# One-hot rows for the gate matmuls: both indices compared in one VectorE instruction and the gate multiplied in by ScalarE, in every second gate step

## The reference, cut to what matters

```
cand = v1 + v2 (16 x 16 sums per head);  top, pos = top_k(cand, 16)
eidx = i1 * 128 + i2 at pos;  gate = softmax(top)          # 8 heads x 16 experts per token
act  = gelu(u[eidx] . h, exact) * gate
y    = sum over the 128 chosen experts of act * v[eidx]
```

## Time and profile before

| | |
|---|---|
| time, median of 3 runs | 1566.21 us (1565.37 to 1568.46) |
| the profiled execution's own time | 1565.81 us |
| its span in the trace | 1563.7 us |
| granted TensorE clock, mean | 0.996 of full speed |
| busy over the span | PE 97%, PEld 82%, DVE 90%, ACT 38%, POOL 32% |
| iterations 27 to 50, where the gate steps lie | about 533 to 721 us of the span |

### The profile page before, as it was taken

How to read it: one execution, slowest core, us unless ns; L and a number is a source line. 1 busy time by engine, 2 the same in 40 slices (tenths; PEclk the granted TensorE clock), 3 DMA queues, 4 the chain that set the end, 5 groups by cost and what they waited for, 6 DMA issues and landing times.

```text
span 1563.7 us, 23267 instructions
## 1 busy us (share of the span) xinstructions
PE 1512.8 (97%) x8404; PEld 1281.7 (82%) x8404; DVE 1401.7 (90%) x2988; ACT 596.5 (38%) x968; POOL 493.3 (32%) x422
## 2 busy tenths in 40 slices
PE   7999999899999999999999999999999999999996
PEld 5455654788899999999898999999999899787885
DVE  5887987799999999995999999999999999989997
ACT  3104431521555445543333333333333333334343
POOL 1000000232010411010555565555555555343330
PEclk9999999999999999999999999999999999999998
DMA  9864232230465788789999999999999999999993
GB/s 325 287 217 148 101 138 59 81 98 38 136 212 154 261 262 256 251 278 313 408 396 396 402 401 410 407 397 398 399 407 404 385 402 375 362 406 377 398 391 121
DMA packets 180570, 455.71 MB, mean 291 GB/s; under 512 B 15020, under 2 KB 81700, under 8 KB 178280
## 3 DMA queue, kind: packets, MB, share of 16 engines
q1 hardware_dynamic: 113600, 231.84, 41.2%
q0 software_dynamic: 57632, 209.78, 34.9%
q10 hardware_dynamic: 9224, 12.62, 2.4%
HBM read 421.63 MB, written 32.25 MB: 290 GB/s over the span
## 4 chain that ended last, share of the span: by engine, by line
PE 55%; DVE 13%; DMA 4%; issue 2%; ACT 1%; DVEq 0%; SPq 0%; POOL 0%; ACTq 0%; POOLq 0%
PE peer_psum L1656 13%; PE peer_psum L1660 7%; PE peer_psum L1716 6%; PE peer_psum L1723 6%; PE peer_psum L1731 6%; PE peer_psum L1668 4%; PE peer_psum L1703 3%; PE peer_psum L1720 3%; PE peer_psum L1726 3%; DVE s_all L1807 2%; DMA s_all<-in_peer_v 2%; PE peer_psum L1641 1%; DVE s_all L1902 1%; DVE s_in L1906 1%; DVE s_all L1904 1%
## 5 line engine op out<-in xcount | busy, mean ns | idle before, releaser
L1656 PE MATMUL peer_psum<-hH,hi_slots 128*128 128x320 f32 x1024 | 307.3, 314 | 5.1 <-ACT hi_slots L1599 2.1
L1656 PE MATMUL peer_psum<-hL,hi_slots 128*128 128x320 f32 x1024 | 302.0, 309 | 0.0
L1527 POOL DMA_INDIRECT hT<-in_peer_u,eidx x128 | 146.6, 1145 | 292.0 <-DVE dots L1798 251.5
L1563 ACT ACTIVATE hi_slots<-s_all 128x1024 fp32r<-128x1024 f32 x128 | 135.9, 1062 | 189.2 <-PE peer_psum L1731 172.0
L1527 POOL DMA_INDIRECT hT<-in_peer_v,eidx x128 | 149.6, 1169 | 177.6 <-DVE s_all L1807 164.7
L1656 PEld LDWEIGHTS peer_psum<-hH,hi_slots 128*128 128x128 f32 x1024 | 192.6, 188 | 9.7 <-issue 5.2
L1656 PEld LDWEIGHTS peer_psum<-hL,hi_slots 128*128 128x128 f32 x1024 | 192.6, 188 | 3.1 <-issue 0.2
L1660 PE MATMUL peer_psum<-hH,lo_slots 128*128 128x320 f32 x1024 | 171.2, 309 | 2.1 <-DVE lo_slots L1845 2.1
L1935 DVE TENSOR_TENSOR lo_slots<-s_all,hi_slots 128x1024 fp32r<-128x1024 f32 x128 | 156.3, 1221 | 17.5 <-ACT hi_slots L1563 15.9
L1807 DVE SCALAR_TENSOR_TENSOR s_all<-hT,coef,s_all 128x1024 f32<-128x1024 f32 x126 | 161.3, 1280 | 3.3 <-DMA hT<-in_peer_v,eidx 2.9
L1660 PEld LDWEIGHTS peer_psum<-hH,lo_slots 128*128 128x128 f32 x1024 | 156.6, 188 | 5.1 <-DVE lo_slots L1845 2.6
(11 more groups left out here) (318 smaller groups left out, 2856.6 us busy)
## 6 DMA issues: line engine op xcount, KB each, us to landing
ring<-in_peer_u SPq DMA_DIRECT2D x128, 512.0 KB
s_all<-in_peer_v SPq DMA_DIRECT2D x128, 512.0 KB
gate_table<-lot SPq DMA_DIRECT2D x16, 1280.0 KB, 7.1
lot<-gate_table SPq DMA_DIRECT2D x16, 1280.0 KB
gelu_table<-s_all ACTq DMA_DIRECT2D x56, 160.0 KB
s_in<-gelu_table SPq DMA_DIRECT2D x56, 160.0 KB
x_sb<-in_w_mod POOLq DMA_DIRECT2D x8, 1024.0 KB, 8.2
lot<-in_peer_wq SPq DMA_DIRECT2D x8, 1024.0 KB, 5.6
```

Source lines behind the costliest of these rows:

```text
L1527: pool.indirect_dma_start(rows_of(j), None, A[table][0], bass.IndirectOffsetOnAxis(eidx[:, k:k + 1], 0)).then_inc(rows_in[j % RG], 16)
L1563: func(H[:, slot_of(w), :], vb[:, w % RING, :], ACT.Copy).then_inc(v_hi, 1)
L1656: mm(ps[:, bank, 0:TD], H[:, b, c * P:(c + 1) * P], h[:, c, T0:T], start=(c == 0 and h is hH), stop=False)
```

## The change

In every second gate step (m odd, 40 of 80), VectorE makes one comparison over 4 x 2 x 128 columns for both indices and no multiplication. ScalarE then multiplies the four rows of the second index by the gate, in place, with four instructions over 128 columns (`gate_rows`). TensorE's step waits for ScalarE (`act_made`) instead of for VectorE. Of the odd steps, one that is first or second in its iteration gets its `gate_rows` between `lead_high` and `gelu`; every later one gets it right before the `stage_gates` of the step two before it. Secondly, VectorE makes the low parts of blocks 35 to 39 as well. The semaphore `y_sq` is renamed to `act_made` and its later waits are moved up by the 40 counts.

```diff
-LOW_BY_DVE = [n for n in range(LEAD) if 25 <= n < 35 or n >= 40]
+LOW_BY_DVE = [n for n in range(LEAD) if n >= 25]
+def by_act(m):
+    return m % 2 == 1
+BY_ACT = sum(by_act(m) for m in range(GSTEPS))
...
+            def gate_rows(m):
+                b, d0 = m % NHOT, GT * m
+                act.wait_ge(hot_dve, m + 1)
+                for k in range(GT):
+                    ins = func(onehot[:, b, k, 1, :], onehot[:, b, k, 1, :], ACT.Copy, scale=selT[:, 2, d0 + k:d0 + k + 1])
+                ins.then_inc(act_made, 1)
...
                 if it + 1 < LEAD and it + 1 not in LOW_BY_DVE:
                     lead_low(it + 1)
+                for m in STEPS[it][:2]:
+                    if by_act(m):
+                        gate_rows(m)
                 gelu(it, 4 + it % 2)
...
                 for m in STEPS[it]:
+                    if m + 2 in STEPS[it] and by_act(m + 2):
+                        gate_rows(m + 2)
                     stage_gates(m)
...
             def gates(m):
-                pe.wait_ge(hot_dve, m + 1)
+                if by_act(m):
+                    pe.wait_ge(act_made, sum(by_act(k) for k in range(m + 1)))
+                else:
+                    pe.wait_ge(hot_dve, m + 1)
...
             def hot_rows(m):
                 if m >= NHOT:
                     dve.wait_ge(g_full, m - NHOT + 1)
+                if by_act(m):
+                    v.tensor_tensor(onehot[:, b, :, :, :], iota[:].unsqueeze(1).unsqueeze(1).broadcast_to([P, GT, 2, P]),
+                                    selT[:, 0:2, d0:d0 + GT].rearrange("p i t -> p t i").unsqueeze(3).broadcast_to([P, GT, 2, P]),
+                                    ALU.is_equal).then_inc(hot_dve, 1)
+                    return
```

More of the change, by code:

```diff
@@ L1419, in peer_block @@
         (u_turned, half_turned, u_high, u_less, u_low, u_low_dve, ua_high, ua_low, ub_high, ub_low, u_done, s_ready, v_hi, v_lo, v_done, c_done,
-         a_ready, a_hi, a_lo, yc_done, folded, y_sq, out_ready) = (sem(n) for n in (
+         a_ready, a_hi, a_lo, yc_done, folded, act_made, out_ready) = (sem(n) for n in (
              "u_turned", "half_turned", "u_high", "u_less", "u_low", "u_low_dve", "ua_high", "ua_low", "ub_high", "ub_low", "u_done", "s_ready",
-             "v_hi", "v_lo", "v_done", "c_done", "a_ready", "a_hi", "a_lo", "yc_done", "folded", "y_sq", "out_ready"))
+             "v_hi", "v_lo", "v_done", "c_done", "a_ready", "a_hi", "a_lo", "yc_done", "folded", "act_made", "out_ready"))
         def rows_of(j):
@@ L1608, in _ @@
                     for h in range(2):
-                        func(y[:, 1, 0:512], y_of(0, h), ACT.Square, accum_out=stat[:, 0, h:h + 1]).then_inc(y_sq, 1)
-                        act.wait_ge(y_sq, h + 1)
+                        func(y[:, 1, 0:512], y_of(0, h), ACT.Square, accum_out=stat[:, 0, h:h + 1]).then_inc(act_made, 1)
+                        act.wait_ge(act_made, BY_ACT + h + 1)
             act.wait_ge(c_done, 1)
@@ L1620, in _ @@
                         act.wait_ge(folded, h + 1)
-                    func(sq[:], y_of(t, h), ACT.Square, accum_out=stat[:, 0, 2 * i + h:2 * i + h + 1]).then_inc(y_sq, 1)
-                    act.wait_ge(y_sq, 2 * i + h + 1)
+                    func(sq[:], y_of(t, h), ACT.Square, accum_out=stat[:, 0, 2 * i + h:2 * i + h + 1]).then_inc(act_made, 1)
+                    act.wait_ge(act_made, BY_ACT + 2 * i + h + 1)
         @block.tensor
@@ L1987, in _ @@
                 if n == FIN + 2:
-                    dve.wait_ge(y_sq, 2)
+                    dve.wait_ge(act_made, BY_ACT + 2)
                     rstd(0, 1)
@@ L1996, in _ @@
                 for h in range(2):
-                    dve.wait_ge(y_sq, 2 * i + h + 1)
+                    dve.wait_ge(act_made, BY_ACT + 2 * i + h + 1)
                     step.put(v.tensor_tensor(y[:, t, h * 512:(h + 1) * 512], y_of(t, h), gg2[:, h * 512:(h + 1) * 512], ALU.mult))
```

## The result

The changed kernel takes 1572.87 us (median of 7 runs, 1571.28 to 1576.53), the kernel before 1566.21 (7 runs beside it, 1562.58 to 1568.46). The ratio is 1.0038 with a 95% interval of 1.0024 to 1.0051, so it is slower by about 6 us (3.8 to 8.0). Forecast were 1573.9, slower, and a range of 1567 to 1579. The profiled execution took 1572.42, with a span of 1570.4.

What follows compares the result with a forecast made beforehand. TensorE's chain was taken to bound the gate stage, with ScalarE lacking slack inside runs of gate steps. 9.9 + 0.8 - 2.3 - 0.7 = +7.7 us, so 1573.9 us, 0.5% slower; range 1567 to 1579.

Steps and rivals of the forecast that it cites:

- TensorE sets the end, and a faster VectorE buys only its waits.: Gate stage: iteration 42's chain is TensorE alone, 7.18 us; its waits for VectorE are 1.4 us by matmuls, 2.2 by loads.
- Four ScalarE instructions take 1.275 us; the wait for the bank binds.: Gate steps: a group takes 1.275 us, and the third step's load waits for the first step's move out of PSUM.
- The estimate of 1.17 for a group: ScalarE's four multiplications: 0.29 us each by the page's fixed cost, without overlap, making the forecast 1.6 us lower.
- 24 groups cost nothing, 16 cost 9.9.: Gate stage: 24 groups lie in idle time ahead of the Gelu; 16 ahead of a move delay TensorE 9.9 us.
- The lower bound beside it: ScalarE's groups: at 0.94 us a group, each delay is 0.34 us shorter, 4.5 us in all.
- rival (a): ScalarE's groups are short, 0.94 us: delays shrink to 5.4 us, sum +2.9, about 1569 us; chance 0.14.
- Iteration 27, 0.8.: Iteration 27: VectorE begins late, so TensorE's second step gets its rows late; 0.8 us lost, between 0.4 and 1.2.
- VectorE's relief, 0.7.: Mainly iterations 33 and 34: VectorE's shorter odd steps give TensorE 0.7 us back, bounds 0 and 2.2.
- The low parts, -2.3, hidden by the first edit alone.: Blocks 35 to 39: TensorE drops matmuls, gaining 2.3 us; VectorE takes on 5.7 us, covered by 5.8 saved.
- ScalarE loses five copies that it made in idle time; nothing comes of it: Blocks 35 to 39: dropping ScalarE's copies of the low parts was claimed to change nothing.
- What follows the stage moves along.: Behind the gate stage: TensorE waits for `gelu_table` stores, 7.45 us each, issued relative to its progress, so later work shifts along.
- Rival (d): Behind the stage: drained DMA queues return stores sooner, giving back up to half the loss, 1566 to 1570 us; chance 0.11.

Runs made afterwards that it cites:

- e8: The changed kernel with the 16 later groups multiplying only two of four rows, two tokens' gates left out; 0.9978 of the kernel before, stage -2.4 us.
- e1: The changed kernel with only the 24 odd steps that are first or second in their iteration going over ScalarE; 0.9995 of the kernel before.
- e2: The changed kernel with only the 16 odd steps that are third or later in their iteration going over ScalarE; 1.0050 of the kernel before.
- e3: The changed kernel with the groups of an iteration's first four steps all ahead of the Gelu; 1.0037 of the kernel before, stage +3.0 us.
- e4: The changed kernel with each later group behind the move of the step two before it, not ahead; 1.0108 of the kernel before.
- e10: The changed kernel without VectorE's low parts of blocks 35 to 39, first groups ahead of ScalarE's low-part copy; 1.0055 of the kernel before.
- e11: The changed kernel with later groups cut into two halves placed apart, fifth steps and some others left to VectorE; 1.0009 of the kernel before.
- e5: The kernel before with only the low parts of blocks 35 to 39 moved to VectorE; 1.0014 of the kernel before, stage +3.2 us.
- e6: The changed kernel with the low parts of blocks 35 to 39 left to TensorE and ScalarE; 1.0077 of the kernel before, stage +12.0 us.

## Why the prediction was right

The verdict, the size and the mechanism came out, by the steps as they were put:

- *TensorE sets the end, and a faster VectorE buys only its waits.* Shown: VectorE's load fell by 3.8 us in 20 and nothing came of it. With short groups (e8) the most that was gained in the stage is 2.4 us.
- *Four ScalarE instructions take 1.275 us; the wait for the bank binds.* Measured 1.27, and the load 0.12 behind the move's end. The estimate of 1.17 for a group, from the page "VectorE: DVE Perf Modes" of the Trainium skill ("The TRN2 errata"), is 0.1 short by this trace; the 0.29 per instruction agrees with the distance of starts, (1.27 - 0.39) / 3.
- *24 groups cost nothing, 16 cost 9.9.* e1 and e2 show the split. The term of 9.9 was a little large: the clean three-step iterations gave 0.59 instead of 0.63, since the move starts 0.60 and not 0.63 later. The lower bound beside it was worked out wrongly: with groups of 0.94 us the same placing leaves 8 x 0.29 + 2 x 0.45 + 4 x 0.35 = 4.6 us of delay and not 5.4, so rival (a) should have stood at +2.1 and not +2.9. Nothing hung on it.
- *Iteration 27, 0.8.* Measured 0.8 in the change's trace, but 0.1 in e1, e3, e4, e8, e10 and e11. VectorE comes late to it in some executions: its first comparison starts 1.90 us after the iteration's start in the two traces compared, and 1.2 after it in those six. VectorE's last wait for a gathered row ends 4.0 us ahead of the iteration's start in these two, and 5.4 or more ahead of it in those six (last section). So it was a term of one execution, and that the execution measured after was as late there as the one before was luck.
- *VectorE's relief, 0.7.* Only iterations 33 and 34 together can be read, +0.2 against a forecast of +0.3.
- *The low parts, -2.3, hidden by the first edit alone.* The size and the dependence are shown by e5 and e10. The half sentence "ScalarE loses five copies that it made in idle time; nothing comes of it" was wrong: with groups behind them, those copies are worth another 3.6 us (e6 against e10). It did not show in the sum because the change has both edits.
- *What follows the stage moves along.* Shown: the difference of 7.5 us at the start of iteration 51 is still 7.5 at that of iteration 56, in the main stage. Rival (d), the loss absorbed by the stores of `gelu_table`, did not happen. Its premise was misread: between 732 and 752 us of the kernel before TensorE does not stand for 7.45 us per store but has two gaps, 1.61 us (for VectorE's low part) and 2.11 (for ScalarE's high part), and the trace after has 1.53 and 2.11. Later the difference moves between 6.7 and 9.0 us and is 6.7 at the end; the medians differ by 6.7 too, where 7.7 were forecast.

In sum 7.7 were forecast, 6.9 are in the trace from iteration 27 to 50 and 3.8 to 8.0 in the runs.

## What to carry to other kernels

An engine that idles half of its time can still have no slack at one place: look at what its instruction there releases and how soon that is needed, not at its busy share. Moving work there is free up to about the length of the gap (here 0.69 us cost 0.02 at most) and paid in full beyond it, and each instruction that waits for a late engine also holds what stands behind it in the queue. An edit that relieves a full engine gains no more than what the engine that sets the end was waiting for it, here 1.4 to 2.2 us in 188.

## What the runs showed of the hardware that was not expected

The spread of the runs isn't where the change is. In the 13 traces the start of iteration 25, ahead of which all these kernels have the same work, lies between 518.5 and 527.8 us, and iteration 25 itself takes 4.4 to 7.1 us. From iteration 51 to the end, again the same work, it is 839 to 848 us. The nine iterations of the change's trace in which no group stands ahead of a move agree with the kernel before to 0.01 us each. A difference of 0.1% between two of these kernels drowns in the medians and can be read in the stage. Iteration 26 of the change's trace, which has no gate step, is 0.85 us longer than before: TensorE waits 0.77 there for a low part that VectorE makes behind a gathered row, whose arrival VectorE waits for (before, then after):

```profile
528.00 1.23 DVE L1798 CUSTOM_DVE_ANT_0 more_rows<-more_rows,lot 128x1024 f32<-128x1024 f32 x1 [2.21 <-DMA more_rows<-in_peer_u,eidx]
528.66 1.23 DVE L1822 CUSTOM_DVE_ANT_0 more_rows<-more_rows,lot 128x1024 f32<-128x1024 f32 x1 [3.07 <-DMA more_rows<-in_peer_u,eidx]
```

So part of this spread is the time at which a gathered row lands. What makes the stretch ahead of iteration 25 differ by 9 us stays open.
